# The window keys' unit in 512-column products into four banks, and the turn of the compressed rows one slot later

## The reference, cut to what matters

```python
def shared_kv(h, kv_w, pos_k, w1_k, w2_k, pos_v, w1_v, w2_v):
    kv = (h @ kv_w).reshape(bsz, seq, 2 * N_BRANCH, N_KV_HEADS, HEAD_DIM)
    k_c, v_c, k_s, v_s, k_w, v_w = [kv[:, :, i] for i in range(2 * N_BRANCH)]
    def compress(t, pos, w1, w2):
        blk = t[:, idx] + pos[None, None, :, None, :]          # 15 blocks of 32 rows, 16 apart
        blk = jnp.moveaxis(blk, 3, 2).reshape(bsz, n_cmp, N_KV_HEADS, CMP_BLOCK * HEAD_DIM)
        return jax.nn.gelu(blk @ w1) @ w2
    return (compress(k_c, ...), compress(v_c, ...), k_s, v_s, k_w, v_w)
```

## Time and profile before

| | |
|---|---|
| time, median of 3 runs | 2002.69 us (2002.27 to 2003.2) |
| profiled execution: its time, its span | 2003.04 us, 2001.2 us |
| TensorE busy | 1989.1 us of the span |
| VectorE, ScalarE, POOL busy | 1314.0, 977.3, 72.8 us |
| mean granted TensorE clock | 0.999 |

### The profile page before, as it was taken

How to read it: one execution, slowest core, us unless ns; L and a number is a source line. 1 busy time by engine, 2 the same in 40 slices (tenths; PEclk the granted TensorE clock), 3 DMA queues, 4 the chain that set the end, 5 groups by cost and what they waited for, 6 DMA issues and landing times.

```text
span 2001.2 us, 31101 instructions
## 1 busy us (share of the span) xinstructions
PE 1989.1 (99%) x11977; PEld 1728.7 (86%) x11977; DVE 1314.0 (66%) x1926; ACT 977.3 (49%) x1439; POOL 72.8 (4%) x84
## 2 busy tenths in 40 slices
PE   9999999999999999999999999999999999999998
PEld 8998889988888888888999988888888888888887
DVE  6998877566666666578767756555555545555555
ACT  5654555354545454455456456544344434434443
POOL 2000122000000000100000001000000000000000
PEclk9999999999999999999999999999999999999999
DMA  9337568546464645756555555566666666666663
GB/s 293 96 133 264 167 202 260 160 136 187 126 194 129 188 144 167 247 154 197 166 168 155 155 168 190 177 188 191 197 189 189 191 192 189 189 197 181 195 192 107
DMA packets 203220, 360.75 MB, mean 180 GB/s; under 512 B 25392, under 2 KB 33936, under 8 KB 202448
## 3 DMA queue, kind: packets, MB, share of 16 engines
q1 hardware_dynamic: 200944, 351.82, 57.1%
q0 software_dynamic: 1664, 5.97, 0.9%
q10 hardware_dynamic: 480, 1.10, 0.1%
HBM read 355.96 MB, written 2.10 MB: 179 GB/s over the span
## 4 chain that ended last, share of the span: by engine, by line
PE 87%; DVE 7%; issue 1%; ACT 1%; POOL 0%; POOLq 0%; DVEq 0%; ACTq 0%
PE acc L533 36%; PE acc L537 9%; PE banks L567 9%; PE acc L567 9%; PE banks L533 8%; PE banks L570 4%; PE acc L570 4%; DVE w_high_low L1864 2%; PE banks L1013 1%; PE banks L986 1%; PE acc L585 1%; PE acc L607 1%; PE banks L999 1%; PE banks L1065 1%; PE banks L1089 0%
## 5 line engine op out<-in xcount | busy, mean ns | idle before, releaser
L1864 DVE TENSOR_TENSOR w_high_low<-raw,w_high_low 128x1024 fp32r<-128x1024 f32 x646 | 791.1, 1233 | 598.9 <-ACT w_high_low L1232 596.3
L1232 ACT ACTIVATE w_high_low<-raw 128x1024 fp32r<-128x1024 f32 x646 | 680.1, 1059 | 710.5 <-PE acc L533 293.4
L533 PE MATMUL acc<-w_high_low,x_high_low 128*128 128x512 f32 x1608 | 387.2, 396 | 0.4 <-DVE w_high_low L1864 0.4
L533 PEld LDWEIGHTS acc<-w_high_low,x_high_low 128*128 128x128 f32 x1608 | 299.4, 188 | 63.2 <-issue 0.8
L533 PE MATMUL acc<-w_high_low,h_high 128*128 128x512 f32 x1088 | 292.1, 390 | 0.2 <-DVE w_high_low L1864 0.2
L537 PE MATMUL acc<-x_high_low,w_high_low 128*128 128x256 f32 x2064 | 261.5, 285 | 0.0
L537 PEld LDWEIGHTS acc<-x_high_low,w_high_low 128*128 128x128 f32 x2064 | 251.7, 191 | 1.8
L567 PE MATMUL acc<-x_high_low,w_high_low 128*128 128x512 f32 x768 | 241.9, 396 | 0.4
L567 PE MATMUL banks<-x_high_low,w_high_low 128*128 128x512 f32 x768 | 241.2, 395 | 0.0
L533 PEld LDWEIGHTS acc<-w_high_low,h_high 128*128 128x128 f32 x1088 | 203.0, 188 | 41.9 <-issue 0.6
L570 PEld LDWEIGHTS banks<-x_high_low,w_high_low 128*128 128x128 f32 x768 | 144.3, 188 | 34.1
(11 more groups left out here) (393 smaller groups left out, 1655.3 us busy)
## 6 DMA issues: line engine op xcount, KB each, us to landing
raw<-in_b_w_in SPq DMA_DIRECT2D x128, 512.0 KB, 3.8
raw<-in_w_mlp_in SPq DMA_DIRECT2D x128, 512.0 KB, 3.7
raw<-in_w_mlp_out SPq DMA_DIRECT2D x128, 512.0 KB, 4.7
raw<-in_w_in SPq DMA_DIRECT2D x96, 512.0 KB, 3.7
raw<-in_kv_w SPq DMA_DIRECT2D x48, 512.0 KB, 4.2
raw<-in_a_w_in SPq DMA_DIRECT2D x32, 512.0 KB, 6.2
raw<-in_b_w_out SPq DMA_DIRECT2D x32, 512.0 KB, 4.6
raw<-in_w_out SPq DMA_DIRECT2D x32, 512.0 KB, 4.7
```

Of the source, the lines that this page charges most:

```text
L533: ins_ = nc.tensor.matmul(PAIRS[pair][:, t, :], xa[:, kt + j, t * P:(t + 1) * P], wa[:, k, j, :], start=first and n == 0, stop=last and n ...
L1232: nc.scalar.activation(WH[:, s % SPLIT, :, :], RAW[:, s, :, :], ACT.Copy).then_inc(hi_ready, ticks_since(base_, p))
L1864: V.tensor_tensor(WL[:, k, :, :], RAW[:, p % SLOTS, :, :], WH[:, k, :, :].bitcast(F32), ALU.subtract).then_inc(lo_ready, ticks_since(base_ ...
```

## The change

The eight `tick` calls of the window keys become `wide_tick` calls, the body of `wide` taken out as a function: the result lies in the two banks of ACC[0] and the two of BANKS[1], as sums in two halves. In the first of them, the block m = 2 is preceded by a wait for acc_free at G_KV+4. ScalarE and VectorE read the result with `keys_high` and `keys_sum` (two instructions each) where each had one. `comp_turn` stands behind slot 2 of its unit where it stood behind slot 1, with a wait of its own for acc_free at G_KV+5, and `comp_hidden` one slot later as well. Transfers are the same.

```diff
@@ TensorE
-                k = s % SPLIT
-                pe.wait_ge(lo_ready, unit * SLOTS + s + 1)
-                for m in range(4):
...
+                wide_tick(unit * SLOTS + s, s, free, pairs)
                 if extras is not None:
                     extras(s)
+
+        def wide_tick(tau, s, free, pairs):
+
+            k = tau % SPLIT
+            pe.wait_ge(lo_ready, tau + 1)
+            for m in range(4):
+                if s == 0 and m % 2 == 0:
+                    pe.wait_ge(acc_free, free[m // 2])
+                both = PAIRS[pairs[m // 2]][:, m % 2, :]
+                for j in range(2):
+                    nc.tensor.matmul(both, WH[:, k, j, m * P:(m + 1) * P], XX[:, 2 * s + j, :, :].rearrange("p c t -> p (c t)"),
+                                     start=s == 0 and j == 0, stop=False, skip_group_check=True)
+                for j in range(2):
+                    ins_ = nc.tensor.matmul(both[:, 0:TOK], WL[:, k, j, m * P:(m + 1) * P], XH[:, 2 * s + j, :],
+                                            start=False, stop=s == SLOTS - 1 and j == 1, skip_group_check=True)
+            ins_.then_inc(slot_used, 1)
...
-            tick(tau + 1, (tau + 1) % SLOTS, "cols", (G_KV + 4) % 2, 2 * n, n == 0, n == SLOTS - 1, XH, XL)
+            wide_tick(tau + 1, n, (G_KV + 3, G_KV + 4), ((G_KV + 4) % 2, 3))
 
         def comp_turn(s):
 
-            if s != 1:
+            if s != 2:
                 return
             pe.wait_ge(comp_act, 2)
+            pe.wait_ge(acc_free, G_KV + 5)
@@ ScalarE
-        unit(first=keys_high)
+        def keys_high(keys, unit_, group):
+            done(SLOTS * (unit_ + 1))
+            for b, pair in enumerate((group % 2, 3)):
+                nc.scalar.activation(keys[:, 2 * b:2 * b + 2, :], PAIRS[pair][:, :, 0:TOK], ACT.Copy).then_inc(act_part, 1)
+
+        unit(first=lambda: keys_high(KS, U_KV + 3, G_KV + 3))
...
         def comp_hidden(s):
-            if s != 2:
+            if s != 3:
...
-        unit(first=lambda: (half_copy(U_KV + 5, G_KV + 4, flat(KW[:, 0:2, :])), comp_rows()), extras=comp_hidden)
+        unit(first=lambda: (keys_high(KW, U_KV + 5, G_KV + 4), comp_rows()), extras=comp_hidden)
@@ VectorE
-        unit(first=keys_sum)
+        unit(first=lambda: keys_sum(KS, G_KV + 3))
...
-        unit(first=lambda: half_copy(U_KV + 5, G_KV + 4, flat(KW[:, 2:4, :])), extras=gate_parts)
+        unit(first=lambda: keys_sum(KW, G_KV + 4), extras=gate_parts)
```

More of the change, by code:

```diff
@@ L2365, in _, with keys_sum @@
         unit(first=lambda: kvc_add(1), extras=kvc_lows(1))
-        def keys_sum():
-            for b, pair in enumerate(((G_KV + 3) % 2, 3)):
+        def keys_sum(all_keys, group):
+            for b, pair in enumerate((group % 2, 3)):
                 part()
-                keys = KS[:, 2 * b:2 * b + 2, :]
+                keys = all_keys[:, 2 * b:2 * b + 2, :]
                 ins_ = V.tensor_tensor(keys, keys, PAIRS[pair][:, :, TOK:], ALU.add)
```

## The result

The changed kernel takes 2005.55 us (median of 20 executions, 2004.66 to 2006.28), the kernel before 2002.73 (20 executions, 2002.22 to 2003.2). The ratio is 1.0013 with a 95% interval of 1.0007 to 1.0019: slower, by less than the 0.2% that counted as no change. The 20 executions lie in two clusters: nine from 2004.66 to 2005.09, eleven from 2005.48 to 2006.28, with nothing between. The forecast of 2004.5 is near the lower one, and the median lies in the upper.

A forecast was written before the change was run, and what follows sets the result against it. TensorE, busy for 1989.1 of 2001.2 us, was taken to bound the kernel. A stall of 2.53 less a gain of 0.71 gave +1.82 us, put on the median: 2004.5 us, range 2003.2 to 2006.6.

The forecast's parts named there:

- The ticks: Eight window-key ticks on TensorE: 192 matmuls become 128, saving 0.71 us, bounds 0.3 to 1.1.
- The wait: First wide tick, block m = 2: TensorE waits for BANKS[1]'s read-out until 318.82, losing 2.53 us, bounds 2.5 to 2.65.
- The handover: From VectorE's end of the second addition to TensorE's first start: 0.05 us.
- POOL's addition: Beside VectorE's subtraction ahead of the selected keys' read-out: blocks it, making the read-out 1.04 us later.
- Rival (c): At the new wait: no stall, 2002.0 us, chance 0.03; with VectorE ahead of POOL, shortened stall 1.5, 2003.5 us, chance 0.06.
- the second copy and addition: Window keys' read-out on ScalarE and VectorE: the extra instructions have a cover of 5 us and cost nothing.
- the ring: Ring of four slots behind the stall: next slot ready near 322.7, needed at 324.9, so nothing late.
- the moved turn: Turn of the compressed rows one slot later: same 32 matmuls, its new wait already met, costs nothing.
- The case with the clock at full: New pause on TensorE: stall without a fall of the clock, 2004.5 us, chance 0.49.
- rival (a): Clock falls in the new pause, costing 1.7 us more, between 0 and 2.3: 2006.2 us, within 0.2%, chance 0.33.
- the likeliest case: Whole kernel: stall less gain without a fall of the clock, 2004.5 us, own range 2003.9 to 2005.1, chance 0.49.
- Rival (b): Same fall at 318.8 us, half clock for 4.4 us or more: slower by more than 0.2%, chance 0.07.

The follow-up runs named there:

- e1: Changed kernel with the selected keys copied and added ahead of the next slot's rounding and subtraction; median 0.80 us under the kernel before.
- e9: e1 with the turn of the compressed rows put back behind slot 1; median 0.72 us under the kernel before.
- e10: The changed kernel timed again, beside the kernel before; median 3.39 us above it, ratio 1.0017.
- e2: Changed kernel with POOL's last addition, and the small transfers behind it, released eight slots later; median 0.73 us above the kernel before.
- e7: Kernel before with only the turn of the compressed rows and the gelu on it one slot later; median 0.15 us under the kernel before.
- e5: Kernel before with the wait for acc_free at G_KV+4 put behind half of the first window-key tick; median 3.70 us above the kernel before.
- e8: Changed kernel with BANKS[1] read out first, acc_free counted behind the second addition, that of ACC[1]; median 3.20 us above the kernel before.
- e4: Changed kernel with ten spare 512-column matmuls into an idle bank in front of the wait; median 1.77 us above the kernel before.
- e6: Kernel before with the wait for acc_free at G_KV+4 put in front of the whole first window-key tick; median 6.37 us above the kernel before.
- e3: Changed kernel with BANKS[1] read out first and acc_free counted behind that first addition; median 1.43 us above the kernel before.

## Why the prediction was right, and where it was off

**The ticks.** Gain forecast 0.71 us, bounds 0.3 to 1.1. e1 and e9, without the wait, have the stage shorter by 0.71 both. The alternation with compressed matmuls, which no row showed, costs nothing: 0.94 us for eight of them as before.

**The wait.** Forecast: m = 2 goes from 316.29 to 318.82, 2.53 us late. Measured: 2.53 in both profiled executions of the changed kernel, with 2.36 us of it idle. The handover took 0.06 us, forecast 0.05. A term was missing: behind the pause the first two 512-column matmuls take 0.56 us (318.28 to 318.84) where they otherwise take 0.46 or 0.47, so 0.1 us more. With it the sum is 2.53 - 0.71 + 0.1 = 1.92, and the stage of e10 has 1.91.

**Why the read-out is late.** As forecast: POOL's addition, 1.04 us, shown by e2. Rival (c)'s shortened stall was forecast at 2003.5, 0.8 us above before; e2, which makes it, is 0.73 above.

**Nothing else.** That the second copy and addition, the ring and the moved turn cost nothing was right: e1, e7 and e9, and the 1649.1 us behind the stage with and without the change.

**The clock.** Here the forecast was off in weight. The case with the clock at full had the higher chance, 0.49 against 0.40 for a fall; in fact it fell in the larger part of the executions, if the upper cluster is read so: 11 of 20, and 9 of 11 in e10. For this reading there are one profiled execution of each cluster of the changed kernel, those of e5 and e8 (both upper, both with 3.4 us at half), e4, where the upper cluster goes with the idleness, and the mean granted clocks: 0.998 in 4 of the 11 and 2 of the 9 upper executions, in none of the lower ones. The difference is at the limit of three digits, so for the other upper executions the fall is inferred. So the median of 2005.55 is nearer to rival (a), forecast at 2006.2, than to the likeliest case's 2004.5, whose own range of 2003.9 to 2005.1 holds the nine lower executions. The sum alone is 1.0 us short of the median; that the range to 2006.6 holds it is owed to the rival.

The price in (a), 1.7 us with bounds 0 and 2.3, measured 1.55 in the stage (e8: 1.57). Between the middles of the two clusters (2004.71 and 2005.82) it is 1.1. Part of the difference can be the start: what lies ahead of the stage varies by 1 us from execution to execution, and in the profiled pair it was 0.47 shorter in the upper one, so that their times are only 1.02 us apart. Whether that holds for the clusters as a whole stays open. The row by which the price was set did not show a fallen clock: the first ten products are at half the later pace, but the granted clock of their stretch is recorded as 1.00 in the kernel before. That 1.7 came so near to 1.55 is luck to that extent:

```profile
1.20:5.80 4.60, 4.60 (x11) 3.22 (x11) 0.29 (x1) 1.28 (x1) 4.51 (x9) 1.00 0.78 215
```

The prediction also had the fall inside the pause. So it was in e5, 0.2 us before the end, and in e6; in the changed kernel's and in e8's profiled execution it came 1.4 and 1.3 us after TensorE had gone on.

The trace had what was needed to weigh this better. The earlier trace rows showed the clock gone 2.0 us after the last matmul, and the new pause is longer; against that stood only a pause of 1.0 us, half as long. The Trainium skill (TensorE: Matmul & The Clock Gate, Why this matters for your kernels) warns of idle gaps above some 3 us; in these runs idle times of 2.4 us do it more often than not and 1.8 us sometimes (if e3's upper group is read as the changed kernel's), and the measurement decides.

**Rival (b),** half pace for 4.4 us or more, did not show in the changed kernel's 31 executions (highest 2006.28 and 2006.67, +3.6 and +3.8). It is real all the same with a longer pause: e6 has 6.8 us.

## What to carry to other kernels

A form that saves instructions on the bounding engine but takes one more buffer is worth its saving only when the buffer's last reader is done in time: put the end of that read-out and the engine's arrival side by side before anything else. Here they were 2.5 us apart for a gain of 0.7, and moving the read-out in front of two conversions that had slack (e1) turned a loss of 2.8 us into a gain of 0.8. An idle time of 2.4 us on TensorE cost more than itself in most executions here, because the clock fell in it or behind it; a wait of 1.3 us had only its own price, and where one lasted longer, spare matmuls kept the price at the wait (e4).

## What the runs showed of the hardware that was not expected

- Idle time of TensorE ahead of the wait's end, and what followed: 1.32 us (e2), one cluster in eleven executions; 1.76 us (e3), two groups, 5 of 11 in the upper; 2.36 us (changed kernel), 11 of 20 and 9 of 11 in the upper; 3.74 us (e6), no execution where a full clock would put it, and no mean granted clock over 0.998.
- The clock needn't fall during the pause: in the changed kernel it fell at 319.7 us, 1.4 us after TensorE had gone on without a break; in e5, after an idle time of the same length, it fell 0.2 us before TensorE went on.
- A fallen clock stayed at half for 3.4 us in the profiled executions of the changed kernel, e5 and e8, and for 6.8 us in e6's, with TensorE busy for 5.5 of them.
- The first two 512-column matmuls behind a pause take 0.1 us more than in the stream, at the full clock too (0.57 us in e2 and e4, 0.56 in e10), and even in e4, where the spare matmuls had ended only 0.04 us earlier.
